# LayerNorms of a two-block transformer kernel: sums of x prepared by VectorE, new x formed by VectorE, the first two products in turns

## What is computed

```python
def layer_norm(x, g, b):
    mu = jnp.mean(xf, axis=-1, keepdims=True)
    var = jnp.mean(jnp.square(xf - mu), axis=-1, keepdims=True)
    y = (xf - mu) * lax.rsqrt(var + LN_EPS)
    return y * g + b

x = layer_norm(x, emb_ln_g, emb_ln_b)                      # n = 0
for l in range(2):
    h = hybrid_mixer(x, ...)                               # ends in w_mix_out, "mo"
    x = layer_norm(alpha * x + h, ln_g[l, 0], ln_b[l, 0])  # n = 1, 4
    h = memory_cross_attention(x, mem, ...)                # ends in xa_o, "xo"
    x = layer_norm(alpha * x + h, ln_g[l, 1], ln_b[l, 1])  # n = 2, 5
    h = conv_ffn(x, ...)                                   # ffn_w_in "fu", "fg"; ffn_w_out "fo"
    x = layer_norm(alpha * x + h, ln_g[l, 2], ln_b[l, 2])  # n = 3, 6
```

## Time and profile before

| | |
|---|---|
| median of 3 runs (lowest, highest) | 2180.6 us (2178.9, 2188.47) |
| profiled execution | 2176.07 us |
| its span, first to last instruction | 2174.3 us |
| mean granted TensorE clock | 0.985 of full |
| TensorE busy (matrix products) | 2093.7 us, 96% |
| VectorE busy | 1430.6 us, 66% |
| ScalarE busy | 1004.3 us, 46% |
| GpSimd busy | 53.2 us, 2% |

### The profile page before, as it was taken

How to read it: one execution, slowest core, us unless ns; L and a number is a source line. 1 busy time by engine, 2 the same in 40 slices (tenths; PEclk the granted TensorE clock), 3 DMA queues, 4 the chain that set the end, 5 groups by cost and what they waited for, 6 DMA issues and landing times.

```text
span 2174.3 us, 39332 instructions
## 1 busy us (share of the span) xinstructions
PE 2093.7 (96%) x17364; PEld 2038.1 (94%) x17364; DVE 1430.6 (66%) x1717; ACT 1004.3 (46%) x1166; POOL 53.2 (2%) x58
## 2 busy tenths in 40 slices
PE   7999999899989999998999799998999999999997
PEld 6899999899988999998999799988999999989997
DVE  6656564577765655646777766698666766887664
ACT  5554454444445444544444454444444544444442
POOL 1000000000000000001000000000000000000000
PEclk9999999999999999999999899999999999999999
DMA  5444554355534444534555355533555555533552
GB/s 206 151 160 159 190 177 154 117 194 194 194 120 155 156 175 175 192 139 147 193 194 194 104 193 195 190 136 119 194 194 194 180 194 192 178 130 132 194 195 83
DMA packets 52858, 365.95 MB, mean 168 GB/s; under 512 B 5904, under 2 KB 5904, under 8 KB 9296
## 3 DMA queue, kind: packets, MB, share of 16 engines
q1 hardware_dynamic: 52272, 361.21, 46.5%
q0 software_dynamic: 416, 2.22, 0.3%
HBM read 362.35 MB, written 1.05 MB: 167 GB/s over the span
## 4 chain that ended last, share of the span: by engine, by line
PE 82%; issue 9%; DVE 5%; ACT 2%; POOL 1%; DMA 1%; POOLq 0%; ACTq 0%
PE accM L1104 47%; PE scoreP L1104 18%; PE outP L1104 8%; PE turnP L1104 8%; DVE wlo L1537 1%; PE turnP L1284 1%; ACT ew L932 1%; ACT whi L747 1%; POOL small L689 1%; ACT x L812 0%; DMA raw<-in_W 0%; PE outP L1310 0%; DVE cen L1633 0%; DVE mrs L2076 0%; DVE cen L1639 0%
## 5 line engine op out<-in xcount | busy, mean ns | idle before, releaser
L1537 DVE TENSOR_TENSOR wlo<-raw,whi 128x2048 fp32r<-128x2048 f32 x336 | 768.4, 2290 | 379.7 <-ACT whi L747 379.1
L747 ACT ACTIVATE whi<-raw 128x2048 fp32r<-128x2048 f32 x336 | 640.1, 1911 | 261.9 <-PE accM L1104 143.6
L1104 PE MATMUL accM<-xh,whi 128*128 128x256 f32 x1152 | 337.2, 293 | 11.2 <-DVE xl L1653 10.7
L1104 PE MATMUL scoreP<-xh,whi 128*128 128x256 f32 x1152 | 323.1, 280 | 13.7 <-DVE xl L1653 8.8
L1104 PE MATMUL accM<-xh,wlo 128*128 128x256 f32 x1152 | 322.8, 280 | 0.0
L1104 PE MATMUL accM<-xl,whi 128*128 128x256 f32 x1152 | 322.8, 280 | 0.0
L1104 PE MATMUL scoreP<-xl,whi 128*128 128x256 f32 x1152 | 321.2, 279 | 0.0
L1104 PE MATMUL scoreP<-xh,wlo 128*128 128x256 f32 x1152 | 320.9, 279 | 0.0
L1104 PE MATMUL accM<-fh,wlo 128*128 128x256 f32 x1056 | 291.5, 276 | 0.0
L1104 PE MATMUL accM<-fh,whi 128*128 128x256 f32 x1056 | 291.5, 276 | 0.0
L1104 PE MATMUL accM<-fl,whi 128*128 128x256 f32 x1056 | 291.5, 276 | 0.0
(11 more groups left out here) (273 smaller groups left out, 4161.0 us busy)
## 6 DMA issues: line engine op xcount, KB each, us to landing
raw<-in_W SPq DMA_DIRECT2D x336, 1024.0 KB, 4.8
biasr<-in_bias SPq DMA_DIRECT2D x16, 256.0 KB, 2.8
raw<-in_memT SPq DMA_DIRECT2D x2, 1024.0 KB, 5.4
cc<-in_consts POOLq DMA_DIRECT2D x1, 1408.0 KB, 6.8
x<-in_xT SPq DMA_DIRECT2D x4, 256.0 KB, 4.5
out<-x SPq DMA_DIRECT2D x4, 256.0 KB, 2.6
c<-in_consts SPq DMA_DIRECT2D x1, 464.5 KB, 6.8
par<-in_par POOLq DMA_DIRECT2D x2, 203.5 KB, 3.6
```

Of the source, the lines that this page charges most:

```text
L747: nc.scalar.activation(whi[:, hi_slot(c), :], raw[:, raw_slot(c), :], ACT.Copy).then_inc(split_hi.sem, 1)
L1104: return nc.tensor.matmul(dst, a, b, start=start, stop=stop, skip_group_check=True)
L1537: v.tensor_tensor(wlo[:, raw_slot(c), :], raw[:, raw_slot(c), :], whi[:, hi_slot(c), :].bitcast(F32), ALU.subtract).then_inc(split_lo.sem, 1)
```

## The change

For each LayerNorm n = 0 to 6 VectorE adds banks 0 and 1 of x into `cen[:, 0]`, then bank 2 (`add_tokens`, signal `xsummed`), and TensorE sums that and bank 3 only: 4 products in place of 8. ScalarE's last square no longer waits for the third addition of squares.

For the LayerNorms n = 0 to 5 (`feeding`) the back is new. VectorE waits for both spreads, works bank 0 in halves of 128x256 (scale, shift, scale, shift), and forms the new x itself (`affine`, two instructions per bank). ScalarE writes only xh, straight from `cen` with g and b. The lower parts of banks 0 and 1 come from VectorE (`lower`), those of 2 and 3 from GpSimd.

On TensorE the first two products behind n = 2, 5 (fu 0, fg 0) and n = 3 (dq 0, dk 0 of the second layer) take turns, two tiles of x at a time (`leads_pair`). Behind n = 0 they do not. The programs of ScalarE, VectorE and SyncE are not changed for the turns.

```diff
@@ -466,13 +473,15 @@
         spread = sig("spread", norms)
         mdiaged = sig("mdiaged", lns)
         mspread = sig("mspread", lns)
-        scaled = sig("scaled", [(n, b) for n in lns for b in range(NB)])
+        feeding = [n for n in fed if n < END1]
+        scaled = sig("scaled", [(n, b) for n in lns for b in range(NB) if b or n not in feeding])
+        centred_half = sig("centred_half", feeding)
         centred = sig("centred", [(n, b) for n in lns + [LAST] for b in range(NB)])
         xnew = sig("xnew", [(n, b) for n in lns + [LAST] for b in range(NB)])
         spread_kept = sig("spread_kept", [n for n in norms if END1 < n < LAST])
         xhi = sig("xhi", [(n, b) for n in fed for b in range(NB)])
-        xlo0 = sig("xlo0", [(n, 0) for n in fed if n <= END1])
-        xlo1 = sig("xlo1", [(n, b) for n in fed if n <= END1 for b in range(1, NB)])
+        xlo0 = sig("xlo0", [(n, b) for n in feeding for b in range(2)])
+        xlo1 = sig("xlo1", [(n, b) for n in feeding for b in range(2, NB)])
         xlo2 = sig("xlo2", [(n, b) for n in fed if n > END1 for b in range(NB)])
         x_in = [sem(f"x_in{b}") for b in range(NB)]
         c0_in = sem("c0_in")
@@ -688,8 +697,9 @@
                 pool.wait_ge(varied.sem, varied.at(n))
                 nc.gpsimd.tensor_tensor(root, var, mhalf, ALU.pow).then_inc(rooted.sem, 1)
                 if n in fed and n <= END1:
-                    for b in range(1, NB):
+                    for b in range(2, NB):
                         pool.wait_ge(xhi.sem, xhi.at((n, b)))
+                        pool.wait_ge(xnew.sem, xnew.at((n, b)))
                         k = slice(2 * b, 2 * b + 2)
                         nc.gpsimd.tensor_tensor(xl[:, k, :], x[:, k, :], xh[:, k, :].bitcast(F32), ALU.subtract)\
                             .then_inc(xlo1.sem, 1)
@@ -767,7 +777,7 @@
 
             def square(n, b):
                 if b >= 2:
-                    act.wait_ge(summed.sem, summed.at((n, b - 1)))
+                    act.wait_ge(summed.sem, summed.at((n, 1)))
                 nc.scalar.activation(sq[:, b % 2, :], x[:, 2 * b:2 * b + 2, :].rearrange("p k s -> p (k s)"),
                                      ACT.Square).then_inc(squared.sem, 1)
 
@@ -797,6 +807,17 @@
                 if late:
                     late()
                 for b in range(NB):
+                    if n in feeding:
+                        for m in range(2):
+                            if b == 0 and m == 0:
+                                act.wait_ge(centred_half.sem, centred_half.at(n))
+                            else:
+                                act.wait_ge(centred.sem, centred.at((n, b)))
+                            g, bb = affine_of(n, 2 * b + m)
+                            ins = nc.scalar.activation(xh[:, 2 * b + m, :], cen[:, b % 2, m * S:(m + 1) * S],
+                                                       ACT.Identity, bias=bb, scale=g)
+                        ins.then_inc(xhi.sem, 1)
+                        continue
                     act.wait_ge(centred.sem, centred.at((n, b)))
                     for m in range(2):
                         k = 2 * b + m
@@ -805,17 +826,10 @@
                             g0 = C0["fin_g"][0] + k
                             ins = nc.scalar.activation(x[:, k, :], src, ACT.Copy, scale=c0[:, g0:g0 + 1])
                         else:
-                            if n == 0:
-                                g, bb = (c0[:, C0[q][0] + k:C0[q][0] + k + 1] for q in ("emb_g", "emb_b"))
-                            else:
-                                g, bb = (col(q, ((n - 1) % 3) * KT + k) for q in ("ln_g", "ln_b"))
+                            g, bb = affine_of(n, k)
                             ins = nc.scalar.activation(x[:, k, :], src, ACT.Identity, bias=bb, scale=g)
                     ins.then_inc(xnew.sem, 1)
-                    if n in fed:
-                        act.wait_ge(xnew.sem, xnew.at((n, b)))
-                        nc.scalar.activation(xh[:, 2 * b:2 * b + 2, :], x[:, 2 * b:2 * b + 2, :], ACT.Copy)\
-                            .then_inc(xhi.sem, 1)
-                    elif n == END1:
+                    if n == END1:
                         act.wait_ge(xnew.sem, xnew.at((n, b)))
                         upper(n + 1, b)
                 if between and n <= END1 and n % LNS != 1:
@@ -1108,10 +1122,12 @@
                 outB.claim(pe, varied, n)
                 if n <= END1:
                     turnB.claim(pe, ysums, n)
-                    for k in range(KT):
-                        if k % 2 == 0:
-                            await_x(pe, n, k // 2)
-                        ins = mm(turnP[:, 0:S], ones[:, :], x[:, k, :], k == 0, k == KT - 1)
+                    pe.wait_ge(xsummed.sem, xsummed.at((n, 2)))
+                    for h in range(2):
+                        mm(turnP[:, 0:S], ones[:, :], cen[:, 0, h * S:(h + 1) * S], h == 0, False)
+                    await_x(pe, n, NB - 1)
+                    for h in range(2):
+                        ins = mm(turnP[:, 0:S], ones[:, :], x[:, KT - 2 + h, :], False, h == 1)
                     ins.then_inc(ystats.sem, 1)
                 for signal, key, src in ((summed, (n, NB - 2), accq), (squared, (n, NB - 1), sq[:, (NB - 1) % 2, :])):
                     pe.wait_ge(signal.sem, signal.at(key))
@@ -1156,7 +1172,7 @@
                         for fn in hooks.get(k, []):
                             fn()
                         if c.get("norm") is not None and k % 2 == 0:
-                            xlo = xlo2 if c["norm"] > END1 else xlo1 if k else xlo0
+                            xlo = xlo2 if c["norm"] > END1 else xlo1 if k >= 4 else xlo0
                             pe.wait_ge(xlo.sem, xlo.at((c["norm"], k // 2)))
                         for m in range(2):
                             first, last = k == 0 and m == 0, k == KT - 1
@@ -1465,6 +1481,9 @@
 
                 return c["role"] == "xo" and name == "back" and what["j"] == c["j"]
 
+            def leads_pair(pos):
+                return pos > 0 and chunks[pos]["role"] in ("dq", "fu") and chunks[pos]["j"] == 0
+
             hooks = {}
 
             def hook(c, k, fn):
@@ -1491,7 +1510,13 @@
                     else:
                         hook(pos, SPREAD * (i - first) // (len(mine) - first),
                              lambda name=name, what=what: step(name, what))
-                product(c, hooks.get(pos, {}))
+                if leads_pair(pos):
+                    other = chunks[pos + 1]
+                    for k in range(0, KT, 2):
+                        product(c, hooks.get(pos, {}), k, k + 2)
+                        product(other, {}, k, k + 2)
+                elif pos == 0 or not leads_pair(pos - 1):
+                    product(c, hooks.get(pos, {}))
                 n = c.get("ends")
                 if n is None or c["role"] == "sd" and c["f"] == 0:
                     continue
@@ -1573,6 +1598,19 @@
                     a = sq[:, 0, :] if b == 1 else accq
                     v.tensor_tensor(accq, a, sq[:, b % 2, :], ALU.add).then_inc(summed.sem, 1)
 
+                def flat(b):
+                    return x[:, 2 * b:2 * b + 2, :].rearrange("p k s -> p (k s)")
+
+                def add_tokens(b):
+                    if b == 1:
+                        for d in range(2):
+                            await_x(dve, n, d)
+                        v.tensor_tensor(cen[:, 0, :], flat(0), flat(1), ALU.add).then_inc(xsummed.sem, 1)
+                    else:
+                        await_x(dve, n, 2)
+                        dve.wait_ge(xsummed.sem, xsummed.at((n, 1)))
+                        v.tensor_tensor(cen[:, 0, :], cen[:, 0, :], flat(2), ALU.add).then_inc(xsummed.sem, 1)
+
                 for b in range(NB):
                     if n in ended:
                         dve.wait_ge(obank.sem, obank.at((n, b)))
@@ -1585,6 +1623,8 @@
                         ins.then_inc(resid.sem, 1)
                     if split_here and b >= 1:
                         lo_part(n, b - 1)
+                    if n in lns and b >= 2:
+                        add_tokens(b - 1)
                     if not split_here and b >= 1:
                         add_squares(b - 1)
                 if split_here:
@@ -1628,7 +1668,9 @@
                     return cen[:, b % 2, :].rearrange("p (m s) -> p m s", m=2)
 
                 def scale(b):
-                    if b >= 2:
+                    if b >= 2 and n in feeding:
+                        dve.wait_ge(xhi.sem, xhi.at((n, b - 2)))
+                    elif b >= 2:
                         dve.wait_ge(xnew.sem, xnew.at((n, b - 2)))
                     v.tensor_tensor(c3(b), bank_of_x(b), ra, ALU.mult).then_inc((centred if rms else scaled).sem, 1)
 
@@ -1638,6 +1680,45 @@
                     dve.wait_ge(scaled.sem, scaled.at((n, b)))
                     v.tensor_tensor(c3(b), c3(b), ma, ALU.subtract).then_inc(centred.sem, 1)
 
```

(43 more changed lines are left out.)

5 lines of the change are left out of this document (added).

## The result

The changed kernel took 2199.41 us (median of 20 runs, 2187.12 to 2213.26), the kernel before 2185.66 us (20 runs, 2173.75 to 2200.5): a ratio of 1.0056, with a 95% interval of 1.0035 to 1.0076. By the ratio that is 12.2 us more, between 7.6 and 16.6; the medians themselves differ by 13.8. Ratios and medians leave out the few executions that ran in the chip's slow state, and the ratios are the estimates that belong to the intervals, so they can differ a little from quotients of medians. Its 2186.3 us stood on a median of 2180.6 from three runs; on that base the measured change makes 2192.8 us, inside the range of 2175 to 2198 and above the forecast's own 2178 to 2191. Rival 2 in full (the clock falls at all six new places, +19.1 us in all) was too dear. The profiled execution took 2191.16 us (span 2189.3), against a span of 2174.3.

A forecast was written before the change was run, and what follows sets the result against it. TensorE, busy 96% of the span, bounds the kernel. Terms 3.0 - 1.0 - 1.5 + 2.5 + 2.5 - 0.2 + 0.4 give +5.7 us, 2186.3 us from a median of 2180.6; range 2175 to 2198.

The forecast's parts named there:

- Rival 2: Sums at n=2, 3, 5, 6 and two down products: clock falls in new idle time, 13.4 us more, 2199.7; chance 0.24.
- a wait of 2.7 at the first down product: Feed-forwards at n=2 and n=5: turns delay fu's copy, splits, conv and fl, so TensorE waits; +2.5 us at each.
- n=0: First LayerNorm: later sums and a later weight split delay the second product, +3.0 us, bounds +1.1 and +4.1.
- n=1: Norm woven into products of memory: 1.5 us earlier, less a 0.5 us wait for wlo, -1.0 us.
- n=4: Norm woven into products of memory, with 0.4 us more slack than at n=1: -1.5 us.
- The restart: TensorE's next product after the norm at n=2: 417.05 against 417.23, so 0.2 us earlier.
- n=3: Turns' delay meets rotations and scores with more air and is hidden: -0.2 us.
- n=6: Last LayerNorm, old back with the new front: +0.4 us.
- the one that kept the clock out of the sum except at n=0: New idle time (2.0 us at four norms, 2.7 at two down products) was given no clock cost in the sum.
- Rival 1: Split chain behind the turns has more air, so no wait for fl: +0.3 us, 2180.9; chance 0.20.
- Rival 3: Additions slip into VectorE's holes, every norm gains 1.7 us, no late splits: -13.9 us, 2166.7; chance 0.05.
- ten slow passes: Sums at n=0: ten passes at about 0.43 us, six at 0.216, ending at 13.2 against 11.95, +1.3 us.

The follow-up runs named there:

- experiment 1: The changed kernel without the turns, the first two products one after the other again: 2191.85 us, ratio 1.0026 to the kernel before.
- experiment 4: The changed kernel with ScalarE splitting the next chunk before it copies fu's bank: 2192.5 us, ratio 1.0029 to the kernel before.
- experiment 6: The kernel before with six memsets of scratch ahead of the first conv of each feed-forward: 2193.71 us, ratio 1.0031.
- experiment 5: The kernel before with the new front (VectorE's additions, halved sums) at n=1 and n=4 only: 2173.14 us, ratio 0.9938.
- experiment 7: The kernel before with unread products in TensorE's idle time at norms n=0, 2, 3, 5, 6: 2178.78 us, ratio 0.9957.
- experiment 12: The changed kernel with 5 unread products ahead of the first down product of each feed-forward only: 2193.79 us, ratio 1.0037 to the kernel before.
- experiment 11: The changed kernel with unread products in TensorE's idle time at norms n=0, 2, 3, 5, 6 and ahead of first down products: 2189.66 us, ratio 1.0010 to before.
- experiment 3: The changed kernel with the old front, TensorE summing all eight tiles of x: 2191.94 us, ratio 1.0023 to the kernel before.
- the second execution: The changed kernel, unchanged, run and profiled once more: 2203.18 us, ratio 1.0103 to the kernel before.

## Why the prediction was right or wrong

**The waits were right in place and size.** The earlier trace rows without a hole gave a wait of 2.0 us ahead of the sums: 1.99. From the first half to the restart 3.8: 3.78. The chain of the earlier trace rows, copy, two splits, conv, fl, gave a wait of 2.7 at the first down product: 2.68, at n=2 and at n=5, and experiments 1, 4 and 6 confirm its cause. n=0 was +3.0, measured +2.86, though the start of the program varies so much that this is in part luck: the second product begins between 30.28 and 31.54 us in five executions with the old norm there (the kernel before twice, experiments 5 to 7), and between 33.14 and 34.02 in five with the new (the changed kernel twice, experiments 1, 4 and 12). n=1 was -1.0, measured -1.34 (the wait for wlo is there and cost 0.15 us in place of 0.5); n=4 -1.5, measured -1.72. The restart was 0.5 us earlier at n=2, 5 rather than 0.2, and the first product, less of it at half clock, gained another 0.48. n=3 was right but for the clock (experiment 12, without the fall, has -0.3 at its restart). n=6 was +0.4 and measured +1.33, with no fall in its sums, and +1.04 in experiment 11: the wait and the sums make 0.33 (1.98 + 3.69 against 5.34), and for the rest no run shows a cause. The affine steps take 0.73 us for two, priced at 0.75; the smaller price set beside it is not borne out. Without the clock the terms add up to +4.9 in the trace (11.0 - 6.1) and +3.9 in the clean pair of experiments 11 and 7, against 5.7.

**The step that failed is the one that kept the clock out of the sum except at n=0.** The sum put the new idle time at nothing beyond its length, and the clock's fall behind it cost about 6 us in the profiled execution. The argument against rival 2, that the clock falls only after longer idle time than 2.0 us, had been drawn from one place, the 2.9 us at 408 to 411 with a fall behind it. The rows could not bear it: they showed what happens after such a wait, and nothing of a shorter one. Measured, waits of 1.9 to 2.7 us are in between: it fell behind all six waits of 2.68 us of the changed kernel (twice) and of experiment 3, behind one of two waits of 1.9 in experiment 6, and in 7 of the 24 sums behind 1.9 to 2.0 us of idle time. The price of one fall was right in rival 2 (1.7 us at a down product; 2.5 in the sums, measured 1.8 and 1.7; 2.4 to 2.6, though only 1.69 of it lies in the sums themselves). It fell at three of the six places, 6.1 us in place of 13.4, and at four in the second execution. By the prediction's own words rival 2 decides from two or three falls or 5 us on; so the mechanism that it gave 0.24 is the one that happened, at half its full price, and the forecast's 0.51 leaned on rows that could not bear it. With 6.1 on top, 5.7 becomes 11.8, next to the measured 12.2; that closeness is partly luck, since the second group of runs has the change at 16.6 to 28.2 us (1.0076 to 1.0129). The Trainium skill ("TensorE: Matmul & The Clock Gate", Part 1), by which the throttled state is the default and activity lifts it, is borne out by experiments 7, 11 and 12: activity in the wait kept the clock.

**Rival 1 fell** (no wait for fl, 2180.9): the wait is there. **Rival 3 fell** at the earlier trace rows.

**At n=0 the low clock was the right reason, and the number of slow passes a guess.** The first four passes take 1.84 us to the start of the next (7.34 to 9.18), and the second four (9.18, 1.91 us, above) stand in the trace just as four passes of the sums of n=3 do, where the clock is recorded at half. TensorE, changed kernel, n=3:

```profile
613.55 1.91 PE L1118 MATMUL turnP<-x,ones 128*128 128x256 f32 x4
```

Either way a pass comes every 0.427 us, twice the 0.216 of later ones. A window over this stretch (7.3 to 11.0) shows a PEclk of 1.00, which is misleading: the trace's record of the clock begins only at 12.18 us, with the level full, and a stretch without a record counts as full. The passes change to 0.216 between 12.16 and 12.39 us, just there. In the kernel before, record and change both lie near 8.6 us, in its second execution near 9.6, and in experiment 11 near 10.7. The sum took ten slow passes from the row; it was 11 in this execution, 13 in the second, 8 in experiment 11. Its bound for all at full clock was a little off: 7.6 + 16 x 0.216 is 11.1 us, 0.9 under 11.95, where it has -0.5.

## What to carry to other kernels

A wait that a change puts on the tensor engine is to be priced twice: its length, and the half clock that may follow it (here 1.7 to 2.6 us for 2 to 2.7 us of waiting). That second price can be had back with products that nobody reads, in exactly that idle time, and so can what the kernel already pays at its old waits: 9 us here by the ratio, 5 by the steps in the trace. Interleaving two products to hide a late operand delays whatever consumes the first one; follow that consumer's queue to its end before counting the gain, and take the cheaper arithmetic (here the additions) only where the tensor engine doesn't wait for it.

## What the runs showed of the hardware that was not expected

- At full granted clock a 128x128 weight load with a 128x256 product comes every 0.1131 or every 0.1175 us, and one of the two holds over stretches of 140 us and more. Which one differs between executions of the same kernel: 26.0 us between two spans of the kernel before, 21.4 between two of the changed one. The difference sought (12 us) is smaller than that, so spans of single profiles don't compare. Medians of 20 runs gave an interval of 9 us, and within profiles only steps at a given wait compare.
- The half clock after a wait isn't a function of its length alone: 1.91 us and 1.90 us in one execution, one with a fall and one without.
- The fall comes late: the clock is full in the wait of 441.99 to 444.67 and half behind 445.7, after TensorE has gone on.
- TensorE's first passes of the program, some 8 to 14 of them, come at 0.427 us, as at the half clock of n=3's sums, and change to 0.216 where the record of the clock begins. A PEclk of 1.00 ahead of that point is no measurement.
- Idle time that a change makes elsewhere can bring a fall too: behind 1.81 and 2.29 us at n=1 in experiments 1 and 4, not behind 0.40 in the changed kernel nor 1.33 in experiment 12.
